# The first down projection ends block by block: four resident contraction tiles at the boundary between two decoder layers

## The reference

```python
def conv_ffn(x, w_up, w_conv, w_down):
    ...
    return (jax.nn.silu(g) * a) @ w_down        # (512, 2816) @ (2816, 1024)

# end of layer A
x = x + conv_ffn(rmsnorm(x, norm_ffn), ffn_up, ffn_conv, ffn_down)
# shared K/V, once
k_flat, v_flat = jnp.split(rmsnorm(h, kv_norm) @ w_kv_shared, 2, axis=-1)
# start of layer B
proj = rmsnorm(x, norm_attn) @ w_in
```

## Time and profile before

| | |
|---|---|
| time, median of 3 runs | 1392.23 us (1390.17 to 1392.29) |
| span of the profiled execution | 1381.4 us |
| time of the profiled execution itself | not shown; the median is 10.8 us above the span |
| PE, DVE, ACT busy | 94%, 59%, 40% of the span |
| the down projection's matmuls | 595.0 to 714.85 us of the span |
| first memory score matmul of layer B | 743.53 us |

### The profile page before, as it was taken

How to read it: one execution, slowest core, us unless ns; L and a number is a source line. 1 busy time by engine, 2 the same in 40 slices (tenths; PEclk the granted TensorE clock), 3 DMA queues, 4 the chain that set the end, 5 groups by cost and what they waited for, 6 DMA issues and landing times.

```text
span 1381.4 us, 17557 instructions
## 1 busy us (share of the span) xinstructions
PE 1294.8 (94%) x6167; PEld 1053.7 (76%) x6167; DVE 815.2 (59%) x1294; ACT 555.4 (40%) x922; POOL 102.6 (7%) x132
## 2 busy tenths in 40 slices
PE   5889999998999999999988897887999999999997
PEld 4767777767788888888866676775878888878886
DVE  5857667754677777742257665555477777772222
ACT  5444444433444444432135432433344444442114
POOL 0201222232100000000020000000300000000000
PEclk9999999999999999999999998989999999999998
DMA  7412111102333333322231131210333333332221
GB/s 218 119 31 62 46 47 46 46 16 77 92 102 95 91 97 101 95 96 99 91 92 46 34 89 31 62 46 19 104 90 92 91 99 98 93 104 92 91 76 61
DMA packets 167122, 109.78 MB, mean 79 GB/s; under 512 B 3414, under 2 KB 159390, under 8 KB 167070
## 3 DMA queue, kind: packets, MB, share of 16 engines
q1 hardware_dynamic: 167070, 109.10, 26.0%
HBM read 106.99 MB, written 2.10 MB: 79 GB/s over the span
## 4 chain that ended last, share of the span: by engine, by line
PE 83%; DVE 10%; ACT 3%; issue 2%; DMA 1%; SPq 0%; DVEq 0%; POOL 0%; ACTq 0%; POOLq 0%
PE bank L1431 17%; PE bank L1194 16%; PE bank L1195 16%; PE bank L1196 16%; PE bank L1409 2%; PE bank L1376 2%; PE bank L1343 2%; PE bank L1344 2%; PE bank L1345 2%; DVE w_lo L779 2%; PE bank L1397 1%; PE bank L1530 1%; PE bank L1486 1%; DVE y_lo L785 1%; PE bank L1378 1%
## 5 line engine op out<-in xcount | busy, mean ns | idle before, releaser
L1194 PE MATMUL bank<-y_hi,w_hi 128*128 128x512 f32 x928 | 371.4, 400 | 8.4 <-DVE y_lo L785 5.9
L1195 PE MATMUL bank<-y_lo,w_hi 128*128 128x512 f32 x928 | 364.2, 392 | 0.0
L1196 PE MATMUL bank<-y_hi,w_lo 128*128 128x512 f32 x928 | 364.0, 392 | 0.0
L779 DVE TENSOR_TENSOR w_lo<-raw,w_hi 128x1024 fp32r<-128x1024 f32 x196 | 240.6, 1227 | 206.7 <-ACT w_hi L487 205.5
L487 ACT ACTIVATE w_hi<-raw 128x1024 fp32r<-128x1024 f32 x196 | 207.0, 1056 | 374.9 <-PE bank L1431 169.2
L1431 PE MATMUL bank<-ar,w_hi 128*128 (+1 forms) x704 | 217.0, 389 | 1.6 <-DVE af L1003 1.6
L1194 PEld LDWEIGHTS bank<-y_hi,w_hi 128*128 128x128 f32 x928 | 176.4, 190 | 49.4 <-DVE y_lo L785 9.0
L1196 PEld LDWEIGHTS bank<-y_hi,w_lo 128*128 128x128 f32 x928 | 175.9, 190 | 37.6
L1195 PEld LDWEIGHTS bank<-y_lo,w_hi 128*128 128x128 f32 x928 | 176.4, 190 | 35.8 <-issue 1.4
L1431 PEld LDWEIGHTS bank<-ar,w_hi 128*128 128x128 f32 x704 | 132.0, 188 | 29.6 <-DVE af L1003 2.4
L1431 PE MATMUL bank<-ar,w_lo 128*128 (+1 forms) x352 | 137.0, 389 | 0.0
(11 more groups left out here) (173 smaller groups left out, 1496.9 us busy)
## 6 DMA issues: line engine op xcount, KB each, us to landing
raw<-in_a_ffn_up SPq DMA_DIRECT2D x44, 512.0 KB, 3.8
raw<-in_b_ffn_up SPq DMA_DIRECT2D x44, 512.0 KB, 3.8
raw<-in_a_ffn_down SPq DMA_DIRECT2D x22, 512.0 KB, 3.2
raw<-in_b_ffn_down SPq DMA_DIRECT2D x22, 512.0 KB, 3.2
raw<-in_a_w_in SPq DMA_DIRECT2D x20, 512.0 KB, 3.7
raw<-in_w_kv_shared SPq DMA_DIRECT2D x12, 512.0 KB, 3.6
raw<-in_a_w_out SPq DMA_DIRECT2D x8, 512.0 KB, 3.5
raw<-in_b_w_in SPq DMA_DIRECT2D x8, 512.0 KB, 3.5
```

The lines of the kernel that those rows point to most:

```text
L779: nc.vector.tensor_tensor(w_lo[:, m % SPLIT, :], raw[:, m % RAW, :], w_hi[:, m % SPLIT, :].bitcast(F32), ALU.subtract).then_inc(lo_done, 1)
L1194: mm(bank, w[0], y[0][:, k, :], start=(k == 0), stop=False)
L1195: mm(bank, w[0], y[1][:, k, :], start=False, stop=False)
L1196: last = mm(bank, w[1], y[0][:, k, :], start=False, stop=(k == KT - 1))
```

## The change

For layer 0 alone, the down projection is cut in two. DX = 4 contraction tiles stay resident, DK = 18 go as before (six written out, then two turns of six). The weights of the last four are split into `wx_hi` and `wx_lo`, which lie over the first 16 pieces of act_hi, as soon as these are used up. Then PE goes through the eight output blocks, and finishes each with its 12 matmuls (`down_last`). Each block has a signal of its own, f_done, and the adds, y_hi, squares, y_lo follow it. The split of the K/V input goes into the same order (Y_B), and `shared_high` and `shared_low` are gone. The splits of tiles 102 and 103 stand ahead of all adds. Layer 1 is unchanged.

```diff
+DX = 4
+DK = FT - DX
+        wx_hi = ar[:, 0:4096].rearrange("p (i d) -> p i d", i=DX)
+        wx_lo = ar[:, 4096:8192].rearrange("p (i d) -> p i d", i=DX)
+        Y_B = [("y", 0)] + [t for k in range(4) for t in (("y", k + 1), ("kv", k))] + \
+            [("y", k) for k in range(5, KT)] + [("kv", k) for k in range(4, KT)]
...
 ScalarE:
-                ring(n_dn + 2)
-                ring(n_dn + 3)
-                with act.Fori(0, 3) as i:
-                    for j in range(6):
-                        ring(i * 6 + (n_dn + 4 + j), n_dn + 4 + j, i)
                 if l == 0:
-                    ring(N_QMB)
-                    for k in range(KT):
-                        absorb(2, k)
-                        if k == 3:
-                            ring(N_QMB + 1)
+                    for j in range(2, 6):
+                        ring(n_dn + j)
+                    with act.Fori(0, 2) as i:
+                        for j in range(6):
+                            ring(i * 6 + (n_dn + 6 + j), n_dn + 6 + j, i)
+                    for i in range(DX):
+                        n = n_dn + DK + i
+                        act.wait_ge(raw_full[n % RAW], 16 * (n // RAW + 1))
+                        act.wait_ge(tile_done, n_dn + 2 * i + 2)
+                        nc.scalar.activation(wx_hi[:, i, :], raw[:, n % RAW, :], ACT.Copy).then_inc(hi_done, 1)
+                    for n in (N_QMB, N_QMB + 1):
+                        act.wait_ge(raw_full[n % RAW], 16 * (n // RAW + 1))
+                        act.wait_ge(tile_done, n_dn + DK + n % SPLIT - 1)
+                        nc.scalar.activation(w_hi[:, n % SPLIT, :], raw[:, n % RAW, :], ACT.Copy).then_inc(hi_done, 1)
+                    for what, k in Y_B:
+                        if what == "y":
+                            absorb(2, k)
+                        else:
+                            nc.scalar.activation(ykv_hi[:, k, :], hT[:, k, :], ACT.Copy,
+                                                 scale=gain(G_KV, k)).then_inc(yhi, 1)
-            shared_high(range(4))
             rms(2)
-            shared_high(range(4, KT))
...
 VectorE:
                 if l == 0:
...
+                    for i in range(DX):
+                        n = n_dn + DK + i
+                        dve.wait_ge(hi_done, n + 1)
+                        dve.wait_ge(tile_done, n_dn + 2 * DX + 2 * i + 2)
+                        nc.vector.tensor_tensor(wx_lo[:, i, :], raw[:, n % RAW, :], wx_hi[:, i, :].bitcast(F32),
+                                                ALU.subtract).then_inc(lo_done, 1)
                     ring(N_QMB)
-                for k in range(KT):
-                    if k < KT - 1:
-                        dve.wait_ge(down_done, 7 * (FT * (l + 1) - 1) + k + 1)
-                    else:
-                        dve.wait_ge(tile_done, n_dn + FT)
-                    nc.vector.tensor_tensor(hT[:, k, :], hT[:, k, :], banks[k][:], ALU.add).then_inc(h_ready, 1)
-                    if l == 0:
-
-                        if k:
-                            absorb_low(2, k - 1)
-                        if k == 4:
-                            ring(N_QMB + 1)
+                    ring(N_QMB + 1)
+                    added = 0
+                    for what, k in Y_B:
+                        while added < min(k + 2, KT) and what == "y":
+                            if added < KT - 1:
+                                dve.wait_ge(f_done, added + 1)
+                            else:
+                                dve.wait_ge(tile_done, n_dn + FT)
+                            nc.vector.tensor_tensor(hT[:, added, :], hT[:, added, :], banks[added][:],
+                                                    ALU.add).then_inc(h_ready, 1)
+                            added += 1
                         dve.wait_ge(h_ready, 16 + k + 1)
+                        if what == "y":
+                            absorb_low(2, k)
+                        else:
+                            dve.wait_ge(yhi, ykv_wait(k))
+                            nc.vector.scalar_tensor_tensor(out=ykv_lo[:, k, :], in0=hT[:, k, :], scalar=gain(G_KV, k),
+                                                           in1=ykv_hi[:, k, :].bitcast(F32), op0=ALU.mult,
+                                                           op1=ALU.subtract).then_inc(ylo, 1)
...
-            shared_low(range(4))
             rms(2)
             for f in range(2):
-                if f:
-                    shared_low(range(4, KT))
                 qk_float(14 + f, N_QMB + f, QSCALE, 1)
...
 TensorE:
+                def down_last(f):
+
+                    for i in range(DX):
+                        k, n = DK + i, n_dn + DK + i
+                        if f == 0:
+                            pe.wait_ge(lo_done, n + 1)
+                            pe.wait_ge(act_lo_done, k + (FT * l + 1))
+                        w = [t[:, i, P * f:P * (f + 1)] for t in (wx_hi, wx_lo)]
+                        for s, (a, b) in enumerate(((w[0], act_hi), (w[0], act_lo), (w[1], act_hi))):
+                            last = mm(banks[f][:], a, b[:, k, :], start=False, stop=(s == 2), skip_group_check=True)
+                        if f == KT - 1:
+                            last.then_inc(tile_done, 1)
+                    if f < KT - 1:
+                        last.then_inc(f_done, 1)
...
+                if l == 0:
+                    for k in range(6):
+                        down(k, n_dn + k, n_dn + k, k == 0)
+                    with pe.Fori(0, 2) as i:
+                        for j in range(6):
+                            down(i * 6 + (6 + j), i * 6 + (n_dn + 6 + j), n_dn + 6 + j, False)
+                    for f in range(KT):
+                        down_last(f)
```

More of the change, by code:

```diff
@@ L320, in y_wait @@
         def y_wait(e, k):
-            return Y0[e] + k + 1
+            return Y0[e] + (Y_B.index(("y", k)) if e == 2 else k) + 1
         def ykv_wait(k):
-            return Y0[2] + KT + k + 1
+            return Y0[2] + Y_B.index(("kv", k)) + 1
         def score_bank(g, hp, i, w):
@@ L665, in ffn @@
                 nc.scalar.preload_act_table_set("natural_log_exp_and_others")
-                ring(n_dn + 2)
-                ring(n_dn + 3)
-                with act.Fori(0, 3) as i:
-                    for j in range(6):
-                        ring(i * 6 + (n_dn + 4 + j), n_dn + 4 + j, i)
-                if l == 0:
-                    ring(N_QMB)
-                    for k in range(KT):
-                        absorb(2, k)
-                        if k == 3:
-                            ring(N_QMB + 1)
+                if l == 0:
+                    for j in range(2, 6):
[19 more added lines that the diff above has]
+                else:
+                    ring(n_dn + 2)
+                    ring(n_dn + 3)
+                    with act.Fori(0, 3) as i:
+                        for j in range(6):
+                            ring(i * 6 + (n_dn + 4 + j), n_dn + 4 + j, i)
             ffn(0, N_UPA, N_DNA)
-            def shared_high(ks):
-                for k in ks:
-                    nc.scalar.activation(ykv_hi[:, k, :], hT[:, k, :], ACT.Copy, scale=gain(G_KV, k)).then_inc(yhi, 1)
-            shared_high(range(4))
             rms(2)
-            shared_high(range(4, KT))
             for f in range(2):
@@ L1030, in ffn @@
                              lambda t, s: conv[:, bass.ds(i * 3 + (base + (2 * t + s) * FT + 1 + j), 1)])
[L1031 to L1035, removed]
-                if l == 0:
-                    ring(N_QMB)
-                for k in range(KT):
-                    if k < KT - 1:
-                        dve.wait_ge(down_done, 7 * (FT * (l + 1) - 1) + k + 1)
-                    else:
-                        dve.wait_ge(tile_done, n_dn + FT)
-                    nc.vector.tensor_tensor(hT[:, k, :], hT[:, k, :], banks[k][:], ALU.add).then_inc(h_ready, 1)
-                    if l == 0:
-                        if k:
-                            absorb_low(2, k - 1)
-                        if k == 4:
-                            ring(N_QMB + 1)
-                        dve.wait_ge(h_ready, 16 + k + 1)
@@ L1051, in ffn @@
-                if l == 0:
-                    absorb_low(2, KT - 1)
+                if l == 0:
+                    for j in range(2, 6):
+                        ring(n_dn + j)
+                    with dve.Fori(0, 2) as i:
+                        for j in range(6):
+                            ring(i * 6 + (n_dn + 6 + j), n_dn + 6 + j)
+                    for i in range(DX):
[4 more added lines that the diff above has]
+                                                ALU.subtract).then_inc(lo_done, 1)
+                    ring(N_QMB)
+                    ring(N_QMB + 1)
[9 more added lines that the diff above has]
+                            added += 1
+                        dve.wait_ge(h_ready, 16 + k + 1)
+                        if what == "y":
+                            absorb_low(2, k)
```

(35 more changed lines are left out.)

1 line of the change is left out of this document (added).

## The result

The changed kernel took 1373.41 us (median of 4 runs, 1369.86 to 1380.56) against 1391.20 us (4 runs, 1385.63 to 1392.29). The forecast's own ratio was 1380.4 / 1392.23 = 0.9915, which is inside the interval.

What follows compares the result with a forecast made beforehand. TensorE, busy 94% of the span, bounds the kernel, so only its waits give time back. Waits of 7.5 us plus 4.3 of half clock save 11.8: span 1369.6, time 1380.4, range 1377.9 to 1384.2 (8 in 10).

Steps and rivals of the forecast that it cites:

- The boundary: From tile 102's start, after layer A's down projection, to layer B's memory scores: 16.9 us instead of 28.7.
- Scores: Layer B's first memory score matmul, forecast to start at 731.7 instead of 743.53.
- tile 104: Layer B's third tile on PE, forecast to start at 728.2 against 739.08, after one wait of about 1.4 us.
- the sum of squares: PE's sum for layer B's first norm, after tile 102's matmuls, forecast at 720.3.
- Rivals 2 to 4: Late weights, under 1 us; weight loads exposed in down_last, 1398.6 us (0.03); sum of squares to scores unshortened, 1383.3 (0.05).
- the tail: From the sum of squares to layer B's memory scores: forecast 11.4 us, against 14.3 in the kernel before.
- Rival 2: down_last's first block waits for late weights of tile 20 or 21: under 1 us, 1381; counted within the forecast's 0.82.
- 10.8 above the span: Whole kernel: median 1392.23 against the profiled span 1381.4, a difference added to the new span 1369.6 to give 1380.4.
- Rival 5: Clock falls added or removed in the stages behind: 2.1 us to both sides; counted within the forecast's 0.82.
- The split of the 11.8 us: Saving before layer B's memory scores: 7.5 us from PE's waits, 4.3 from matmuls at half clock.
- The value x: VectorE time for each y_lo and kv_lo in the new block order: taken as 1.18, costing from 1.3.
- rival 1: VectorE's queue becomes the bound in the block stage: 1 to 6.2 us, 1381.5 to 1386.6; over 2 us at 0.10.

Runs made afterwards that it cites:

- thin squares: GpSimd adds one column of squares instead of 512 for layer B's first norm; first down matmul to memory scores: 144.74 us (kernel before), 136.68 (changed kernel).
- put back: Changed kernel with the K/V input split where it stood before, four blocks ahead of rms and four behind; the run took 1370.82 us.

## Why the prediction was right and wrong

**The boundary: right, to 0.1 us.** Scores at 731.80 for 731.7; blocks 2.72 us apart; down_last at 0.227 a matmul (96 between 693.2 and 714.7) with no wait in front; clock 1.00; tile 104 at 728.22 for 728.2, with a wait of 1.36 for 1.4; the sum of squares at 720.35 for 720.3. B has this size in all three profiles of the kernel. Rivals 2 to 4 did not come: there is no wait at down_last, its matmuls are at full pace, and the tail is 11.45 us long, not 14.3. Rival 2 was nearer than forecast: the last low part of the resident weights ends at 693.0 and not at 691.4, 2.1 us before PE needs it (695.13). That the whole span agrees, 1369.8 for 1369.6, is in part luck: the two profiled executions that it compares both had a clock of 0.91 in A, and another execution of the changed kernel has a span of 1383.2.

**The absolute time: wrong.** The step that failed is the one between span and time. The prediction took "10.8 above the span" as time that lies around the span. In every execution on record the two lie 1.7 to 2.0 us apart (1371.64 and 1369.8, 1384.32 and 1382.5). The 10.8 was a difference between two executions: the profiled one took about 1381.4 + 1.8 = 1383.2 us (an estimate from these runs), and the median of three stood in the upper part of a scatter of 1378.5 to 1393.0. From 1383.2, the sum gives 1371.4; the profiled execution of the changed kernel took 1371.64.

**The range: its term for the clock was too small.** Rival 5 took 2.1 us, the spread of three runs. Over all runs the kernel before spreads by 14.5 us and the changed one by 16.3, and three profiles of the latter put 11.9 us of that in layer B's attention, where the granted clock is 0.91 or 0.88 with nearly the same waits. What decides how often an execution falls stays open: these runs show the falls, and that surplus matmuls lower their share, but not why two executions of the same program differ in them. With this scatter the three ratios of the changed kernel, 0.9891, 0.9925 and 0.9903, all hold 0.9915 within their intervals, and of the 17.8 us between the first two medians about 6 are chance: 11.8 us is what the change does in B. The means of all 68 runs of the kernel before and all 23 of the changed one, 1386.3 and 1374.9, lie 11.4 us apart.

**The split of the 11.8 us: right as a count of TensorE's time, wrong as causes.** The prediction gave 7.5 us to waits and 4.3 to half clock. TensorE's idle time in the stretch did fall by 7.6 us (8.96 to 1.36) and its busy time by 4.2 (19.72 to 15.53). But half clock was not worth 4.3: the surplus matmuls in the kernel before remove 5.5 us of it ahead of the sum of squares, tile 104 starts 1.45 us earlier, and 0.66 us is left at the scores. The causes that experiments carry are others. GpSimd's contention is 3.8 us (thin squares). The K/V split in the tail is 2.1 (put back). The rest, 11.8 - 3.8 - 2.1 = 5.9 us, is found by subtraction, as if the parts simply add: VectorE's work moved under the last contraction tiles, and in it what half clock cost. No run here separates these two.

**The value x: the right side, for another reason.** The prediction took 1.18, and 0.75 came; up to 1.3 it cost nothing. The Trainium skill, "GPSIMD Engine Reference", section "Key points", names VectorE instructions with two SBUF inputs as those that contend; the runs agree (w_lo 2.30 to 1.23 and y_lo 1.18 to 0.75 with thin squares, the bank adds at 0.67 to 0.69 throughout). But the prediction took every y_lo and kv_lo as exposed. When VectorE waits for each bank, its two-input operations are over before the square of the same block reaches GpSimd, and the next thing beside GpSimd's 1.30 us is an idle VectorE and a bank add. With half the time per block this order is lost, and the price is 6.3 us. That rival 1 had 6.2 for x = 1.87 is a coincidence: four of the eight y_lo in that run take 1.16 to 1.19 us.

## What to carry to other kernels

A product that keeps all its accumulators open to the last contraction tile hands its consumers everything at once. A few resident tiles at the end, enough that one block lasts longer than the vector work on it, give time back at no cost to TensorE; here with too few the vector engine ran late and fell into contention. Before a forecast of an absolute time, find out which execution the profile shows: its span, what lies around it, and how far executions of one program lie apart; and in a kernel with such scatter read small steps from the length of a stretch in the trace, not from the total. What is taken off one engine's end has to be charged where it goes: sums set between the blocks shortened the end by 10.6 us and the kernel by 5.

## What the runs showed of the hardware

Two executions of one program differed by 13.6 us (1371.41 and 1384.97); 11.9 of them lie in one stretch, where the engines other than TensorE had equal work in equal time and TensorE's granted clock was 0.91 or 0.88. And a TensorE kept at full clock ahead of a wait (1.00 instead of 0.81) gained 1.45 us of 5.5 us less half clock where the chain ran through VectorE, and 0.66 us after the fall of the clock had moved behind it: in these runs a low granted clock in a row is a price only as far as TensorE is what the next step waits for.
